# A second place for x, 192 bytes off a 256-byte line, and all weights of the seven-product slabs on the line

## The reference

```python
h = x
h = h + 0.5 * swiglu(rms_norm(h, g1), w1, w3, w2)      # ffn1: 1024 -> 2816 -> 1024
h = h + mixer(rms_norm(h, gm))                         # dilated attention, pooling, gates
h = h + 0.5 * swiglu(rms_norm(h, g2), w1b, w3b, w2b)   # ffn2, the same shapes
x2 = rms_norm(h, gf)
h = x2 + rms_norm(retention(rms_norm(x2, ...)))        # second block, first half
h = h + rms_norm(stick_breaking(rms_norm(h, ...)))     # second block, second half
# swiglu(x, w1, w3, w2) = (silu(x @ w1) * (x @ w3)) @ w2
```

## The kernel before, in words

| product | PSUM | stationary, before | moving, before | stationary, changed | moving, changed |
|---|---|---|---|---|---|
| 1: a11 x b11 | acc | 192 (w) | 0 (x) | 0 | 192 |
| 2: s3 x t3 | acc | 0 (w) | 192 (xt) | 0 | 192 |
| 3: s2 x t2 | acc | 0 (w) | 192 (xt) | 0 | 192 |
| 4: a12 x b21 | att | 192 (wc) | 0 (x) | 0 | 192 |
| 5: s1 x t1 | acc | 0 (w) | 192 (xt) | 0 | 192 |
| 6: a22 x t4 | acc | 192 (wc) | 0 (x) | 0 | 192 |
| 7: s4 x b22 | acc | 192 (wc) | 0 (x) | 0 | 192 |
| full slabs, ffn1 | acc | 0 | 0 | 192 | 192 |
| full slab 66 | acc | 0 | 0 | 0 | 192 |
| full slabs 67, 68 | acc | 0 | 0 | 192 | 192 |
| down-projection | acc | 0 (w) | 0 (g) | 0 | 0 |

## Time and profile before

### The profile page before, as it was taken

How to read it: one execution, slowest core, us unless ns; L and a number is a source line. 1 busy time by engine, 2 the same in 40 slices (tenths; PEclk the granted TensorE clock), 3 DMA queues, 4 the chain that set the end, 5 groups by cost and what they waited for, 6 DMA issues and landing times.

```text
span 1875.0 us, 26603 instructions
## 1 busy us (share of the span) xinstructions
PE 1860.3 (99%) x10599; PEld 1626.1 (87%) x10599; DVE 1294.7 (69%) x1728; ACT 867.4 (46%) x1132; POOL 46.5 (2%) x60
## 2 busy tenths in 40 slices
PE   9999999999999999999999999999999999999997
PEld 7998998888888888988998888888888888888886
DVE  8875887887566578866888746364646786666666
ACT  6643664436353236633653242333336654454445
POOL 0000000000000000000000000000000000000000
PEclk9999999999999999999999999999999999999999
DMA  6734763311112235744753223221221222212213
GB/s 212 184 126 123 194 169 110 117 59 62 61 62 93 98 112 141 190 145 115 190 153 123 98 83 107 72 89 67 93 89 66 90 71 87 90 67 89 89 67 90
DMA packets 44382, 203.61 MB, mean 109 GB/s; under 512 B 5136, under 2 KB 6192, under 8 KB 32128
## 3 DMA queue, kind: packets, MB, share of 16 engines
q1 hardware_dynamic: 37088, 177.23, 27.6%
q0 software_dynamic: 6768, 24.50, 6.8%
q10 hardware_dynamic: 432, 0.56, 0.1%
HBM read 198.60 MB, written 3.67 MB: 108 GB/s over the span
## 4 chain that ended last, share of the span: by engine, by line
PE 96%; DVE 2%; ACT 1%; issue 0%; DMA 0%; DVEq 0%; ACTq 0%
PE acc L2205 22%; PE acc L2207 22%; PE acc L2206 22%; PE acc L2212 6%; PE acc L2211 6%; PE acc L2213 6%; PE att L2205 2%; PE att L2206 2%; PE att L2207 2%; PE att L2211 1%; PE att L2213 1%; PE att L2212 1%; PE acc L2442 1%; PE acc L2467 1%; DVE w_lo L1232 0%
## 5 line engine op out<-in xcount | busy, mean ns | idle before, releaser
L1232 DVE TENSOR_TENSOR w_lo<-raw,w_hi 128x2048 fp32r<-128x2048 f32 x126 | 286.9, 2277 | 76.6 <-ACT w_hi L580 75.8
L2205 PE MATMUL acc<-x_hi,w_hi 128*128 128x512 f32 x808 | 318.3, 394 | 0.9 <-DVE x_lo L1295 0.6
L2207 PE MATMUL acc<-x_hi,w_lo 128*128 128x512 f32 x808 | 314.9, 390 | 0.0
L2206 PE MATMUL acc<-x_lo,w_hi 128*128 128x512 f32 x808 | 314.7, 389 | 0.0
L580 ACT ACTIVATE w_hi<-raw 128x2048 fp32r<-128x2048 f32 x126 | 239.2, 1899 | 128.6 <-PE acc L2207 113.9
L2205 PEld LDWEIGHTS acc<-x_hi,w_hi 128*128 128x128 f32 x808 | 151.7, 188 | 36.0 <-issue 2.1
L2206 PEld LDWEIGHTS acc<-x_lo,w_hi 128*128 128x128 f32 x808 | 151.8, 188 | 32.4 <-issue 1.4
L2207 PEld LDWEIGHTS acc<-x_hi,w_lo 128*128 128x128 f32 x808 | 151.7, 188 | 31.9
L2205 PE MATMUL acc<-g_hi,w_hi 128*128 128x512 f32 x352 | 137.0, 389 | 0.0
L2206 PE MATMUL acc<-g_lo,w_hi 128*128 128x512 f32 x352 | 137.0, 389 | 0.0
L2207 PE MATMUL acc<-g_hi,w_lo 128*128 128x512 f32 x352 | 136.9, 389 | 0.0
(11 more groups left out here) (440 smaller groups left out, 4485.1 us busy)
## 6 DMA issues: line engine op xcount, KB each, us to landing
raw<-in_ret_head SPq DMA_DIRECT2D x24, 1024.0 KB, 4.8
raw<-in_ffn_down SPq DMA_DIRECT2D x32, 704.0 KB, 4.0
raw_c<-in_ffn_seven SPq DMA_DIRECT2D x37, 512.0 KB, 5.3
raw<-in_ffn_seven SPq DMA_DIRECT2D x33, 512.0 KB, 4.6
raw<-in_ffn_seven POOLq DMA_DIRECT2D x33, 512.0 KB, 7.5
raw<-in_ffn_seven SPq DMA_DIRECT2D x37, 256.0 KB, 4.5
raw<-in_mix_gate SPq DMA_DIRECT2D x8, 1024.0 KB, 4.8
raw<-in_ret_out SPq DMA_DIRECT2D x8, 1024.0 KB, 4.8
```

The source lines that it names most:

```text
L1232: tt(w_lo[:, slot, at:at + cols], raw[:, slot, 0:cols], w_hi[:, slot, at:at + cols].bitcast(F32), ALU.subtract).then_inc(w_ready, 1)
L2205: mm(dst, still[0], move[0], start=first, stop=False)
L2206: mm(dst, still[0], move[1], start=False, stop=False)
L2207: return mm(dst, still[1], move[0], start=False, stop=last)
```

## The change

x gets one buffer, `x_all`, of which `x_hi` and `x_lo` are the view from element 0, and `xf_hi` and `xf_lo` the view from element 48 (192 bytes). Everything that ffn1 and ffn2 read as x is written to and read from the second view; the mixer, retention and stick-breaking keep the first. In the seven-product slabs the padding between the parts of a slab goes away (`lone` is gone, W_SUMMED is contiguous behind W_LONE), and `to_line_6` goes, so that `wc_hi` and `wc_lo` start on a line. `first_col` now also gives 48 for the full slabs 0 to 3, 67 and 68. `diag_neg` gets a place of its own, so that the tensors behind it stay on a line.

The instructions of every engine, their order, shapes and waits stay as they were; only addresses differ (and with them the names `x_hi` and `x_lo`, which in the new program's rows are both `x`).

```diff
-W_SUMMED = slice(2 * QUART + 64, SLAB + 64)
+W_LONE, W_SUMMED = slice(0, 2 * QUART), slice(2 * QUART, SLAB)
...
+OFF = 48
+FIRST = slice(OFF, OFF + SLAB)
+UP_2 = 67
...
-        x_hi = sb("x_hi", [P, DC, TOK], F32R)
-        x_lo = sb("x_lo", [P, DC, TOK], F32R)
+        x_all = sb("x", [P, 2 * DC * TOK + LINE], F32R)
...
+        def x_from(first):
+
+            both = x_all[:, first:first + 2 * DC * TOK].rearrange("p (s c q) -> p s c q", s=2, c=DC)
+            return both[:, 0, :, :], both[:, 1, :, :]
+
+        x_hi, x_lo = x_from(0)
+        xf_hi, xf_lo = x_from(OFF)
...
-            return LINE * 3 // 4 if values else 0
+            return OFF if values or k < FULL[0] or UP_2 <= k < UP_2 + FULL[1] - 1 else 0
...
-            sb("to_line_6", [P, 48], F32, scope)
...
-                nc.scalar.activation(lone(w_hi, slot), raw[:, slot, cols].rearrange("p (k q) -> p k q", k=2), ACT.Copy).then_inc(w_hi_ready, 1)
+                nc.scalar.activation(w_hi[:, slot, W_LONE], raw[:, slot, cols], ACT.Copy).then_inc(w_hi_ready, 1)
...
-                        weigh(x_hi, 4 * i + (2 * j + o), gains[:, 2, :])
+                        weigh(xf_hi, 4 * i + (2 * j + o), gains[:, 2, :])
...
-                s2, a11, s1, s3 = ((w_hi[:, slot, at:at + QUART], w_lo[:, slot, at:at + QUART]) for at in
-                                   (0, QUART + LINE * 3 // 4, 2 * QUART + LINE, 3 * QUART + LINE))
+                s2, a11, s1, s3 = ((w_hi[:, slot, at:at + QUART], w_lo[:, slot, at:at + QUART]) for at in range(0, SLAB, QUART))
...
-                b11, b21, b22, t4 = ((x_hi[:, rows, cols], x_lo[:, rows, cols]) for rows, cols in
+                b11, b21, b22, t4 = ((xf_hi[:, rows, cols], xf_lo[:, rows, cols]) for rows, cols in
...
-                    pair(at, between)
-                    pair()
+                    pair(at, between, xf)
+                    pair(x=xf)
                 for _ in range(2, full):
-                    pair()
+                    pair(x=xf)
```

More of the change, by code:

```diff
@@ L134, in block_kernel @@
         mean_d = sb("mean_d", [P, P])
+        with ExitStack() as under:
+            diag_neg = sb("diag_neg", [P, P], F32, under)
         rot_r = sb("rot_r", [P, P], F32R)
@@ L178, in value_slot @@
             return head if g == 0 else GROUP_HEADS * (1 + head // 2) + 2 * (g - 1) + head % 2
-        def lone(v, slot):
-            return v[:, slot, 0:2 * (QUART + LINE * 3 // 4)].rearrange("p (k q) -> p k q", k=2)[:, :, 0:QUART]
         def pair_place(slot, ahead):
@@ L302, in block_kernel @@
                 sb("kv_room", [P, 2 * DC, TOK], F32, under)
-                diag_neg = sb("diag_neg", [P, P], F32, under)
                 sq_tok = sb("sq_tok", [P, TB], F32, under)
@@ L669, in form_fourth @@
             def form_fourth():
-                split_val(x_hi[:, 0:TB, LATE], form_b[:])
+                split_val(xf_hi[:, 0:TB, LATE], form_b[:])
             def gate_up(since):
@@ L774, in _ @@
                     act.wait_ge(raw_landed[0] if q == PARTS - 1 else first_landed[q], 16)
-                    nc.scalar.activation(quarter(w_hi[:, 0, 0:SLAB], q), quarter(raw[:, 0, :], q), ACT.Copy).then_inc(
+                    nc.scalar.activation(quarter(w_hi[:, 0, FIRST], q), quarter(raw[:, 0, :], q), ACT.Copy).then_inc(
                         w_hi_ready if q == PARTS - 1 else w_part_ready, 1)
                 act.wait_ge(x_landed[c], 16)
-                weigh(x_hi, c, gains[:, 0, :])
+                weigh(xf_hi, c, gains[:, 0, :])
                 if c == 1:
@@ L786, in _ @@
             for q in range(PARTS):
-                nc.scalar.activation(quarter(w_hi[:, 1, 0:SLAB], q), quarter(raw[:, 1, :], q), ACT.Copy).then_inc(
+                nc.scalar.activation(quarter(w_hi[:, 1, FIRST], q), quarter(raw[:, 1, :], q), ACT.Copy).then_inc(
                     w_hi_ready if q == PARTS - 1 else w_part_ready, 1)
@@ L1338, in low_one @@
                 dve.wait_ge(w_hi_ready, n.at(1))
-                tt(lone(w_lo, slot), raw[:, slot, cols].rearrange("p (k q) -> p k q", k=2), lone(w_hi, slot).bitcast(F32),
+                tt(w_lo[:, slot, W_LONE], raw[:, slot, cols], w_hi[:, slot, W_LONE].bitcast(F32),
                    ALU.subtract).then_inc(w_ready, 1)
@@ L1388, in low_fourth @@
             def low_fourth():
-                low(x_lo[:, 0:TB, LATE], form_b[:], x_hi[:, 0:TB, LATE], forms_ready)
+                low(xf_lo[:, 0:TB, LATE], form_b[:], xf_hi[:, 0:TB, LATE], forms_ready)
             def last_rows(plain):
@@ L1525, in first_low @@
                     dve.wait_ge(w_hi_ready, n.at(1))
-                tt(quarter(w_lo[:, slot, 0:SLAB], q), quarter(raw[:, slot, :], q), quarter(w_hi[:, slot, 0:SLAB], q).bitcast(F32),
+                tt(quarter(w_lo[:, slot, FIRST], q), quarter(raw[:, slot, :], q), quarter(w_hi[:, slot, FIRST], q).bitcast(F32),
                    ALU.subtract).then_inc(w_ready if q == PARTS - 1 else first_ready, 1)
@@ L1535, in _ @@
                 dve.wait_ge(x_landed[c], 16)
-                weigh(x_lo, c, gains[:, 0, :], x_hi)
+                weigh(xf_lo, c, gains[:, 0, :], xf_hi)
             n.next()
@@ L1786, in _ @@
                         add_square(h[:, c, :], False)
-                        weigh(x_lo, c, gains[:, 2, :], x_hi)
+                        weigh(xf_lo, c, gains[:, 2, :], xf_hi)
             final, ret = gains[:, 3, :], gains[:, 4, :]
@@ L2243, in mean_square, with pair @@
                 mm(dst, mean[:], ssq[:], start=True, stop=True).then_inc(att_full, 1 + skip)
-            x = (x_hi, x_lo)
-            def pair(wait=None, between=None):
+            x, xf = (x_hi, x_lo), (xf_hi, xf_lo)
+            def pair(wait=None, between=None, x=x):
                 w = slab()
@@ L2280, in first_pair @@
                     for o in range(2):
-                        block = slice((o * DC + c) * BLK, (o * DC + c + 1) * BLK)
-                        last = passes(dst[o], (w_hi[:, slot, block], w_lo[:, slot, block]), (x_hi[:, c, :], x_lo[:, c, :]), c == 0, c == DC - 1)
+                        block = slice(OFF + (o * DC + c) * BLK, OFF + (o * DC + c + 1) * BLK)
+                        last = passes(dst[o], (w_hi[:, slot, block], w_lo[:, slot, block]), (xf_hi[:, c, :], xf_lo[:, c, :]), c == 0, c == DC - 1)
                         if c == DC - 1:
```

## The result

The changed kernel takes 1883.66 us, the median of 5 runs (1882.95 to 1883.92), beside 1876.59 for the kernel before on the same chip (5 runs, 1876.24 to 1876.79). The ratio is 1.0037, with a 95% interval of 1.0026 to 1.0048: slower by 7.07 us, where 7.2 were forecast. The span grew from 1875.0 to 1880.7 us at an unchanged granted clock of 0.998.

The account below looks back on a forecast made before the run. PE, busy 99% of the span, was taken to bound the kernel. Four slow stages +7.0 us and slab 66 +0.2 us, ACT, DVE and `diag_neg` 0, sum to +7.2 us: from 1876.59 to 1883.8 us, range 1869.3 to 1885.0.

Parts of the forecast that it names:

- PE bounds, only its spacing counts: Whole kernel: PE busy 99% of the span; ACT, DVE and DMA matter only if they make PE wait.
- All four stages slow, +7.0 us: Seven-product slabs, 37 in four stages: each enters and stays at 117.8 ns a matmul, 9.895 us a slab; chance 0.43.
- the old entry: Stage entry in the kernel before, weights 192 loaded under 0: first product slow, 1.41 us in place of 1.36.
- all fast: Rival, seven-product slabs: all four stages at 113.3 ns a matmul, 1869.8 us; chance 0.30.
- No meeting, no change of pace: Inside a stage: pace changes only where next weights load from the phase being streamed; without such meetings the entry pace holds.
- equal phases: Matmul operands: stationary and moving blocks at the same address phase, such as 0 and 0 or 192 and 192.
- Slab 66, +0.2 us: Slab 66, 48 matmuls of 512 columns at phases 0 and 192: 4 ns more each, bounds -0.4 to +0.6 us.
- ACT, DVE and `diag_neg` at 0: Copy at L629 in one part, 1048 ns for 1052, hidden by ACT's idle time; `diag_neg` the same DMA elsewhere: 0.
- the 0.83 us of cover: Seven-product slab: time between the end of ACT's copy and product 5, which waits for it; fast pace takes 0.05 us.
- No effect: Rival, seven-product slabs: weight loads and moving reads don't touch, paces come from products' positions; 1876.6 us; chance 0.04.
- Stages apart: Rival: stages one and three fast, the others slow, 1878.2 us, or the other way round, 1875.5; chance 0.17.
- Worse than slow: Rival, seven-product slabs: a third pace of 120 ns a matmul, 6.8 us more, 1890.6 us; chance 0.04.

Follow-up runs that it names:

- full_0: Changed kernel with the full slabs 0 to 3, 67 and 68 of ffn1 and ffn2 also at 0, x at 192, no spare matmul: 1882.38 us.
- kick_b: Changed kernel plus short spare matmuls (weights 0, x 192) at the four stage entries: one of 64 columns, one, two, three of 128: 1876.26 us.
- fast_wc192: Changed kernel plus one 256-column spare matmul at each stage entry, and third weight part `wc` back at 192: 1886.59 us.
- wc_192: Changed kernel with the third weight part `wc` (products 4, 6 and 7) put back at 192, x still at 192: 1887.57 us.
- all_fast: Changed kernel plus one 256-column spare matmul at each stage entry, weights at 192 (stages 1, 3) or 128 (2, 4), x at 192: 1871.34 us.
- equal: Changed kernel with all weights of the seven-product slabs at 192, `wc` included though meant to stay at 0; x at 192: 1891.36 us.

## Why the prediction was right, point by point

**PE bounds, only its spacing counts: right.** PE's busy time grew by 6.4 us; ACT's grew by 1.5 without a wait in any slab of the changed kernel, and DVE's stayed.

**All four stages slow, +7.0 us: right in mechanism and size.** 9.89 us a slab in all 37, from the forecast 9.895. The traces put 6.95 us between the kernels by the end of stage four, slab 66 and the start-up included. That stage two would repeat "to the letter" held. For stages one and three the nearest row was the old entry, and it held too; but `full_0` shows that it need not have: there stage one is entered fast without a spare. That the direction came out is in part luck: all slow had 0.43 and all fast 0.30, nothing in the trace before could tell stages one and three, and the range took in both cases. So is the agreement of 7.2 with 7.07: by the starts of matmuls the two traces are only 6.95 - 0.42 = 6.5 us apart once stick-breaking is counted.

**"No meeting, no change of pace": right, with a narrower ground than I gave.** Inside a stage at 0 and 192 no run of any kernel changed its pace from the second slab on. But I read the meeting as what turns PE in either direction. The runs show two things: a product of equal phases runs at 120.0 ns, ends the fast pace and leaves 117.8 behind it (`fast_wc192`, `wc_192`), and a break in the spacing may turn it (`kick_b`), also without a meeting.

**Slab 66, +0.2 us: right.** It took 0.27 more, inside the bounds of -0.4 to +0.6. Its first 18 matmuls, on PE's timeline of the changed kernel:

```profile
705.81 0.39 PE L2211 MATMUL acc<-x,w_hi 128*128 128x512 f32 x1
...
710.01 1.02 PE L2249 MATMUL att<-ssq,mean_d 128*128 128x512 f32 x2
```

(710.01 - 705.81) / 18 = 233.3 ns, 6.6 more than the 226.7 of equal phases, where I took 4.

**ACT, DVE and `diag_neg` at 0: right for this kernel.** My remark that at the fast pace the 0.83 us of cover is not used up was wrong for four slabs. I read it from a slab in the middle; the last slab of a stage has another order on ACT, and there a wait costs 0.17 us, as `all_fast` shows.

**What I did not forecast:** the 0.42 us given back in stick-breaking, by a stretch whose addresses did not change. Its first starts in the changed kernel:

```profile
1502.51 0.28 PE L2211 MATMUL acc<-w_hi,kv_hi 128*128 128x256 f32 x1
...
1503.10 0.28 PE L2213 MATMUL acc<-w_hi,kv_lo 128*128 128x256 f32 x1
...
1513.41 0.39 PE L2211 MATMUL att<-sp_hi,sv_hi 128*128 128x512 f32 x1
```

The first five spacings are (1503.10 - 1502.51) / 5 = 0.118 us, the rest 0.113: the stretch turns fast, where before it stayed slow. The other traces bear on it: the addresses of this stretch are the same in all ten kernels, and it takes 117.8 ns a matmul in three of them (before, `kick_b`, `equal`) and 113.5 to 113.6 in the other seven. So it is tipped by something other than its own addresses. I infer that the state reaches it from earlier work or timing; no run tested it, and the 0.42 us can't be counted on as a part of the change.

**The rivals.** "All fast" did not happen but could be had, and near its forecast: 1869.8, and 1871.34 measured, with 0.5 us of the spares and 0.7 of the last slabs in it. "No effect" is refuted in both directions, by 1.0037 and by 0.9971: what the Trainium skill says in "TensorE: Matmul & The Clock Gate", Part 2, step 1, that loading the next weights takes no read bandwidth from the running matmul, is not what decides here, where one set of instructions differs by 7.07 us with the start addresses alone, and the changed one by 12.3 us with four extra matmuls. That reads of SBUF are what collides is my reading of it; the runs show only that phases and history matter. "Stages apart" was seen in `full_0`, with stage one alone fast. "Worse than slow" was seen only at equal phases (`equal`, 1891.36 us); at 0 and 192 no run shows the third pace.

## What to carry to other kernels

Where PE is the bound, read the spacing of its starts stretch by stretch, and compare stretches of one shape. If there are two spacings, the layout may hold a state that is kept and not chosen: then it pays to make the phases of a stage uniform only together with something that sets the state at its entry, and one extra matmul can be enough. A layout that mixes good and bad states, as the one before did, can beat a uniform one that is caught in the bad state.

## What the runs showed of the hardware that was not expected

- The paces are exact steps. With 256 columns, each matmul with its own weight load, they are 113.3, 117.8 and 120.0 ns: 340, 353.3 and 360 ns for three. With 512 columns they are 226.7 ns at equal phases and 233.3 at phases 0 and 192, the latter in some stretches as 231 and 236 in turn.
- Equal phases are the fastest at 512 columns and the slowest at 256.
- At phases 0 and 192 with 256 columns two of the three paces occurred, by what came before: 113.3 in `all_fast`, 117.8 in the changed kernel. 120.0 occurred only inside products at equal phases, and always there: products 4, 6 and 7 of `wc_192` and `fast_wc192`, all seven of `equal`. Equal here means 192 and 192; at 0 and 0 these kernels have only stretches of a few matmuls of 256 columns.
- One spare matmul with its stationary block at 128, or one at 192 and 192 behind matmuls at 192 and 192, turned the pace fast at each of the stage entries where it was tried, seven for the one and seven for the other; one at 0 and 0 behind 0 and 0 did not (once).
